# Second blocks that begin with the latent input, and blocks that begin and end by token block

## The reference

```python
def second_layer(x, ...):
    h = rmsnorm(x, norm_w)
    (m_cq, m_ckv, m_kr, m_gate, g_q, g_k, g_v, g_z, g_b, g_a,
     c_q, c_k, c_v, c_gate) = jnp.split(h @ w_in, split_points, axis=-1)
    y_mla = mla_mixer(m_cq, m_ckv, m_kr, ...) * silu(m_gate)
    y_gdn = gdn_mixer(g_q, g_k, g_v, g_z, g_b, g_a, ...)
    y_moba = moba_mixer(c_q, c_k, c_v, t5_table) * silu(c_gate)
    return x + concatenate([y_mla, y_gdn, y_moba]) @ w_out
```

## Time and profile before

| | |
|---|---|
| median of 3 runs | 1325.55 us |
| profiled execution, its own time | 1327.21 us |
| its span, first to last instruction | 1325.4 us |
| mean granted clock of TensorE | 0.997 |
| TensorE busy | 1301.4 us |
| VectorE busy | 1026.0 us |
| ScalarE busy | 746.5 us |
| weights and data read | 220.88 MB |

### The profile page before, as it was taken

The page is one execution under the profiler, slowest core; times in us unless marked ns, Lnnn a source line. Parts: engine busy times, 40 slices in busy tenths (PEclk is TensorE's granted clock), DMA queues, the critical chain, the costliest instruction groups (busy, mean ns, idle before and its releaser), DMA issues. The chain is left out here.

```text
span 1325.4 us, 26400 instructions
## 1 busy us (share of the span) xinstructions
PE 1301.4 (98%) x10796; PEld 1240.3 (94%) x10796; DVE 1026.0 (77%) x1763; ACT 746.5 (56%) x1149; POOL 47.3 (4%) x48
## 2 busy tenths in 40 slices
PE   9999999999999999999999999999999999999997
PEld 8899999999999999999999989999989899888996
DVE  6899998677777677999997768777778746677565
ACT  6544566556454465544757556544567445586364
POOL 0000000000000000100000000000001100001100
PEclk9999999999999999999999999999999999999999
DMA  8565455565555465646365555665654223343232
GB/s 279 190 201 181 160 161 189 163 220 186 196 191 191 153 229 176 215 162 197 126 210 167 197 184 178 207 203 193 206 163 152 64 97 128 122 143 112 81 101 75
DMA packets 108991, 223.62 MB, mean 169 GB/s; under 512 B 6180, under 2 KB 17700, under 8 KB 108872
## 3 DMA queue, kind: packets, MB, share of 16 engines
q1 hardware_dynamic: 106736, 218.99, 49.5%
q10 hardware_dynamic: 2136, 2.96, 0.7%
HBM read 220.88 MB, written 1.06 MB: 167 GB/s over the span
## 5 line engine op out<-in xcount | busy, mean ns | idle before, releaser
L1191 ACT ACTIVATE whi<-ring 128x1024 fp32r<-128x1024 f32 (+3 forms) x430 | 433.7, 1027 | 343.2 <-PE bank L513 221.3
L1764 DVE TENSOR_TENSOR wlo<-ring,whi 128x1024 fp32r<-128x1024 f32 (+3 forms) x430 | 496.9, 1180 | 166.0 <-ACT whi L1191 133.1
L513 PE MATMUL bank<-hhi,whi 128*128 128x256 f32 x2016 | 272.5, 277 | 2.5 <-ACT hhi L1228 1.8
L522 PE MATMUL bank<-hhi,wlo 128*128 128x256 f32 x2016 | 273.0, 277 | 1.0 <-DVE wlo L1764 1.0
L513 PE MATMUL bank<-hlo,whi 128*128 128x256 f32 x2016 | 269.1, 276 | 0.0
L513 PEld LDWEIGHTS bank<-hhi,whi 128*128 128x128 f32 x2016 | 248.3, 192 | 5.5 <-issue 3.9
L522 PEld LDWEIGHTS bank<-hhi,wlo 128*128 128x128 f32 x2016 | 246.9, 192 | 4.9 <-issue 3.2
L513 PEld LDWEIGHTS bank<-hlo,whi 128*128 128x128 f32 x2016 | 247.3, 193 | 0.0
L1932 DVE SCALAR_TENSOR_TENSOR w<-w,par 128x256 f32<-128x256 f32 x240 | 98.1, 479 | 0.0
L535 PE MATMUL bank<-whi,hhi 128*128 128x512 f32 (+2 forms) x256 | 93.1, 366 | 0.0
L535 PE MATMUL bank<-whi,hlo 128*128 128x512 f32 (+2 forms) x256 | 92.6, 364 | 0.0
(11 more groups left out here) (311 smaller groups left out, 1549.1 us busy)
## 6 DMA issues: line engine op xcount, KB each, us to landing
ring<-in_w_in SPq DMA_DIRECT2D x100, 1024.0 KB, 5.1
ring<-in_w_ffn_down SPq DMA_DIRECT2D x22, 1024.0 KB, 5.1
ring<-in_w_ffn_gate SPq DMA_DIRECT2D x20, 1024.0 KB, 5.1
ring<-in_w_ffn_up SPq DMA_DIRECT2D x20, 1024.0 KB, 5.2
ring<-in_w_merge SPq DMA_DIRECT2D x8, 1024.0 KB, 5.2
ring<-in_w_out SPq DMA_DIRECT2D x8, 1024.0 KB, 5.0
ring<-in_w_oc SPq DMA_DIRECT2D x4, 1024.0 KB, 5.3
ring<-in_w_od SPq DMA_DIRECT2D x4, 1024.0 KB, 5.2
```

What stands on the lines that cost most here:

```text
L513: done = e.matmul(o, wh[:, k, cols(u)], paired(s_[:, k0 + k, :]), stop=False, skip_group_check=True, start=opens and k == 0 and s_ is sh a ...
L522: done = e.matmul(o, wl[:, k, cols(u)], paired(sh[:, k0 + k, :]), start=False, stop=closes, skip_group_check=True)
L1191: e.activation(part_of(whi, j), part_raw(j), ACT.Copy).then_inc(*up("hi.a"))
L1764: e.tensor_tensor(part_of(wlo, j), part_raw(j), part_of(whi, j), ALU.subtract).then_inc(*up("lo.v"))
```

## The change

What it does:

- The order of a second block's input is `m0`, `kc`, `cqk`, `qc`, `vc`, `mg`, `cvg`, `z`. The eight gate columns are columns 416 to 423 of `m0`; the part `ba`, its products and the turning of its result are gone. `TWO_PLAN` has new places for all steps; `MIX_PLAN` is the same.
- The first group of each block takes all four parts' high products for token block 0 first, then for token block 1 (`chans_first`, `toks_first`); the transposes of token block 1 lie inside.
- A block ends by token block over its last two pairs of parts (`last_pairs`); the next block's transposes of token block 0 lie before the last part.
- The norm is done by token block, on 128x512 at a time, with gains read as rows (`rowg`, a 512 KB transfer per norm on ScalarE's queue). Fillers are left at the start of the kernel only.
- High and low activations of the first channel groups go to two halves of a bank, which ScalarE copies and VectorE adds.
- A group takes a bank when its first product needs it (`Held`). The normalization of probabilities (`probs_v`) is a step of its own, after the next logits.
- The bias inputs are loaded during the last feed-forward block.

The core of the diff:

```diff
-TWO_IN = (("kc", 1184, 1696), ("ba", 2720, 2728), ("qc", 672, 1184), ("m0", 0, 416), ("vc", 1696, 2208),
-          ("cqk", 2728, 3240), ("cvg", 3240, 3752), ("mg", 416, 672), ("z", 2208, 2720))
+TWO_IN = (("m0", 0, 424), ("kc", 1192, 1704), ("cqk", 2728, 3240), ("qc", 680, 1192), ("vc", 1704, 2216),
+          ("mg", 424, 680), ("cvg", 3240, 3752), ("z", 2216, 2728))
...
-        "bias": [5, 5, 5, 6],
-        "taps": [12, 20, 34],
-        "others": [28, 34, 41, 41, 53],
-        "decay": [10, 10, 11, 12],
-        "delta": [17, 18, 20, 20, 30, 30, 36, 37, 39, 41, 43, 46, 46, 48, 48, 50, 51, 52, 53, 54, 55, 62, 65, 66, 66],
-        "latent": [26, 29, 30, 34, 36, 37, 39, 43, 46, 53, 54, 65, 66],
-        "outs": [58, 66, 71, 71],
+        "bias": [4, 5, 6, 7],
+        "taps": [16, 33, 41],
+        "silu": [19, 36, 44],
+        "others": [38, 42, 47, 48, 51],
+        "decay": [8, 11, 12, 13],
+        "delta": [22, 23, 25, 25, 28, 29, 32, 33, 35, 37, 39, 41, 43, 45, 46, 48, 49, 50, 52, 53, 54, 60, 63, 64, 64],
+        "latent": [9, 16, 20, 27, 31, 34, 40, 44, 46, 52, 55, 62, 63],
+        "outs": [57, 65, 69, 69],
...
+            def turn_norm(name, l, tb):
+                for g in range(2):
+                    bk = ps.take(e, "s", "nT", name, l, tb, g)
+                    e.wait_ge(*at("xn", name, l, tb, g))
+                    for i in range(4):
+                        done = turn(bk[:, cols(i)], xn[:, tb, cols(4 * g + i)])
...
+            def last_pairs(j, acc, pairs, tag, l, following):
+                for tb in range(2):
+                    for n, ((sh, sl), k0, ready) in enumerate(pairs):
+                        for nh in range(2):
...
+                            elif n == 1 and nh == 1 and following:
+                                turn_norm(*following, 0)
...
+            def chans_first(j, held_of, name, l, mid, after):
...
+                for i in range(4):
+                    e.wait_ge(SEM["hi.a"], j + i + 1)
+                    e.wait_ge(*at("hlo", name, l, 0, i // 2))
+                    products(i, 0, (0, 1))
+                    if i == 3 and not begins:
+                        turn_norm(name, l, 1)
+                    products(i, 0, (2, 3))
+                for i in range(4):
+                    e.wait_ge(*at("hlo", name, l, 1, i // 2))
+                    products(i, 1, range(4)).then_inc(*up("first.p"))
+                    mid(j + i)()
+                    low_ready(j + i)
...
+            def toks_first(j, held, n, name, l, mid, after):
...
+                for i in range(4):
+                    e.wait_ge(SEM["hi.a"], j + i + 1)
+                    e.wait_ge(*at("hlo", name, l, 0, i // 2))
+                    high(i, 0)
+                low_ready(j)
+                low(0, 0)
+                turn_norm(name, l, 1)
...
             def decay_p(l):
-                yield 0
-                bk = ps.take(e, "s", "bg", l)
-                e.wait_ge(*at("rows8", l))
-                for tb in range(2):
-                    done = turn(bk[:, 8 * tb:8 * tb + 8], rows8[:, cols(tb)])
...
                 yield 2
                 bk = ps.take(e, "s", "gsum", l)
-                awake(bk, 6)
                 e.wait_ge(*at("gv", l))
...
+            def norm_a(name, l, x_in, j0):
+                square_a(name, l, x_in, 0)
+                split_to(j0 + 2)
+                high_a(name, l, 0, 0)
+                high_a(name, l, 0, 1)
+                square_a(name, l, x_in, 1)
+                split_to(j0 + 3)
+                scale_a(name, l, xn)
+                high_a(name, l, 1, 0)
+                high_a(name, l, 1, 1)
...
+                for nh in range(2):
+                    add(0, nh)
+                    weigh(0, nh)
                 sums_v(name, l, 0)
+                for g in range(2):
+                    scale_v(name, l, 0, g, xn)
+                split_to(j0)
+                add(1, 0)
+                low_v(name, l, 0, 0)
+                add(1, 1)
+                low_v(name, l, 0, 1)
                 sums_v(name, l, 1)
+                weigh(1, 0)
+                weigh(1, 1)
+                scale_v(name, l, 1, 1, xn)
+                split_to(j0 + 1)
+                low_v(name, l, 1, 0)
+                split_to(j0 + 2)
+                low_v(name, l, 1, 1)
...
                         logits_v(name, l, tb, tag, lgm, 1.0, (mask_mla, mask_moba)[i], 96 + 16 * tb, rowtiles=i == 1)
+                        if tb:
+                            probs_v(name, l, 0, tag, lgm, 96)
+                    yield 7 + 4 * i
+                    probs_v(name, l, 1, tag, lgm, 112)
```

More of the change, by code:

```diff
@@ L574, in norm_p @@
-            def norm_p(name, l):
-                e.wait_ge(SEM["init.v"], 1)
-                for tb in range(2):
[L578 to L588, removed]
+            def turn_norm(name, l, tb):
+                for g in range(2):
+                    bk = ps.take(e, "s", "nT", name, l, tb, g)
+                    e.wait_ge(DMA["id"], 16)
+                    e.wait_ge(*at("xn", name, l, tb, g))
+                    for i in range(4):
+                        done = turn(bk[:, cols(i)], xn[:, tb, cols(4 * g + i)])
+                    done.then_inc(*up("norm.p"))
+                    put("norm.p", "nT", name, l, tb, g)
@@ new lines, in toks_first, with high, low @@
+            def toks_first(j, held, n, name, l, mid, after):
+                def high(i, tb):
+                    wh = part_of(whi, j + i)
+                    for k in range(2):
+                        for s_ in hh:
+                            done = e.matmul(held[tb][:, 0:n], s_[:, 2 * i + k, cols(tb)], paired(wh[:, k, 0:n]), stop=False,
+                                            start=i == 0 and k == 0 and s_ is hhi, skip_group_check=True)
+                    return done
+                def low(i, tb):
+                    wl = part_of(wlo, j + i)
+                    for k in range(2):
+                        done = e.matmul(held[tb][:, 0:n], hhi[:, 2 * i + k, cols(tb)], paired(wl[:, k, 0:n]), start=False,
+                                        stop=i == 3, skip_group_check=True)
+                    return done
+                for i in range(4):
[4 more added lines that the diff above has]
+                low(0, 0)
+                turn_norm(name, l, 1)
+                for i in range(4):
+                    e.wait_ge(*at("hlo", name, l, 1, i // 2))
+                    high(i, 1).then_inc(*up("first.p"))
+                    mid(j + i)()
+                    low_ready(j + i)
+                    if i:
+                        low(i, 0)
+                    low(i, 1).then_inc(*up("second.p"))
+                    after(j + i)
@@ L758, in mix_p @@
                 for name, kind, n, _ in MIX_IN:
-                    held = [ps.take(e, "m", name, l, i) for i in range(2)]
+                    if name == "glu_b":
+                        chans_first(j, lambda u: ps.take(e, "m", name, l, u), "mix", l, between, behind)
+                        j += 4
+                        put("second.p", name, l)
+                        continue
+                    held = [ps.take(e, "s" if name == "glu_a" else "m", name, l, i) for i in range(2)]
                     for i in range(4):
[L761 to L764, removed]
+                        (chans if kind == "chans" else toks)(j, held, n, hh, 2 * i, i == 0, i == 3, between(j))
                         behind(j)
@@ L2204, in ffn_v @@
                         last = [None] * 2
-                        e.wait_ge(*at("gpad", l, i6, i))
+                        if i6:
+                            e.wait_ge(*at("gpad", l, i6, i))
+                        else:
+                            for u in range(2):
+                                g2 = two(gpad[:, i, u, 2:258])
+                                e.wait_ge(*at("gate_high", l, 2 * i + u))
+                                e.tensor_tensor(g2, g2, sides(bank("gate", l, 0, 2 * i + u))[1], ALU.add).then_inc(*up("ffn.v"))
+                                leave("ffn.v", "gate", l, 0, 2 * i + u)
+                            e.wait_ge(*now("ffn.v"))
                         for k3 in range(3):
```

480 lines of the change are left out of this document (263 added, 217 removed).

## The result

The changed kernel takes 1370.59 us (median, 1369.44 to 1372.61), the one before 1326.33: a ratio of 1.0333 with an interval of 1.0313 to 1.0353, so 44 us slower. Forecast was slower, at 1349 with a range up to 1358. The sign and the waits were right; the size was not.

The account below looks back on a forecast made before the run. TensorE, busy 98% of the span, was taken as the bound. Removed work and old waits (-19.1), new waits (+42.2) and clock (0) made net +23.1 on 1325.55, so 1349 us; range 1310 to 1358.

Parts of the forecast that it names:

- (a): Decay sums, place 12: TensorE waits 4.2 us for its operand, 5.2 in layer 0; 9.4 over both layers.
- (b): First inverse step, place 28: TensorE waits 1.3 us for VectorE's queue; 2.6 over both layers.
- (e): Second delta block, place 54: waits 1.7 us for the state's copy behind a split; 3.4 over both layers.
- (f): Second bank of `z`: waits 4.8 us for ScalarE's copy of the first values behind exponentials; 9.6 over both layers.
- (c): Fourth inverse product, place 43: waits 5.4 us for a ScalarE and VectorE chain ending in a subtraction; 10.8 over both layers.
- (d): Turned probabilities, place 44: wait 2.6 us for token block 1's split-off normalization; 5.2 over both layers.
- (g): Place 62: waits 0.6 us for the last normalization; 1.2 over both layers.
- Rival C: Clock adds: six waits over 4 us each bring a half-clock stretch of 1.7 us, net +7, 1355 us; chance 0.12.
- A: Table holds: ScalarE and VectorE come early enough, all new waits vanish, the saved 19.1 stay, 1306 us; chance 0.20.
- B: Half of the waits: only (a), (f) and scraps, 19 to 24 us; 1325 to 1330, no difference; chance 0.13.
- D: Boundaries don't gain: ScalarE's square of token block 1 is held up by a split (1.06); 1353 us; chance 0.05.
- E: Token block 0's high products wait for both blocks' norms, boundaries cost 3 us more each; 1363 us; chance 0.02.

Follow-up runs that it names:

- run 8: The kernel before, with its old input order and blocks, given a new table of places from the same search walk: 1324.6 us, ratio 0.9987.
- run 6: The changed kernel with only another table of places, found by a search over a walk of all engines: 1307.7 us, ratio 0.9871 to the kernel before.
- run 2: The changed kernel with fillers that fit: 20 before the decay sums, 9 before the third inverse product, 19 before z's first product: 1357.4 us.
- run 5: The changed kernel with a table of places made by hand, each long wait taken apart by moving a step or two: 1358.7 us, ratio 1.0239.
- run 4: The changed kernel with latent step 10, the other attention's logits for token block 1, at place 56 instead of 55: 1359.0 us, ratio 1.0241.
- run 1: The changed kernel with fillers before four long waits of each second block (40, 18, 34, 38), each taking twice the time assumed: 1390.9 us.
- run 7: The changed kernel with a second searched table of places, which misplaces two bias steps so it computes something else: 1309.6 us, ratio 0.9880.

## Why the prediction was wrong, point by point

**Boundaries, +1.15 us each, right.** The same product of the two first layers starts at 178.84 and 658.10 before:

```profile
178.84 0.91 PE L513 MATMUL bank<-fhi,whi 128*128 128x256 f32 x6 [1.04 <-DVE w L2178]
658.10 0.57 PE L513 MATMUL bank<-fhi,whi 128*128 128x256 f32 x3 [1.04 <-DVE w L2178]
```

and after:

```profile
179.08 0.68 PE L521 MATMUL bank<-fhi,whi 128*128 128x256 f32 x4 [1.05 <-DVE w L2320]
656.01 0.68 PE L521 MATMUL bank<-fhi,whi 128*128 128x256 f32 x4 [1.04 <-DVE w L2320]
```

Two boundaries lie between: 479.26 against 476.93, 1.17 us each. The result is right, but the working behind it is not: the terms of the chain that the forecast lists add up to 5.8 us, not to "some 5.1". The trace shows why the smaller sum came out all the same:

```profile
311.70 0.69 DVE L1877 TENSOR_TENSOR x<-bank,x 128x512 f32<-128x512 f32 x1 [0.28 <-PE bank L589]
...
313.26 1.29 DVE L1937 TENSOR_TENSOR xn<-x,rowg 128x512 f32<-128x512 f32 x2
313.42 0.95 POOL L2744 TENSOR_TENSOR st<-st,mhalf 128x1 f32<-128x1 f32 x1 [5.40 <-DVE st L1883]
...
316.57 0.69 DVE L1890 TENSOR_TENSOR hboth<-bank,hboth 128x512 fp32r<-128x512 f32 x1 [0.29 <-ACT hboth L1279]
```

Only one addition stands in the chain and the weighing runs beside GpSimd's power, while that power takes 0.95 us for 0.56. From 311.70 to 317.26 it is 5.56 us, against 5.1 and 0.5 of handing over: luck, in part. The boundaries in front of the second blocks, forecast at 0.7 each, were not read apart; TensorE waits 1.0 us for the low halves in each (L644 waiting for L1890, 2.0 in both), where the forecast left 2.0.

The first norm was forecast to cost 0.3. The same product starts 0.24 us later than before in this pair. But over all profiled runs with the new blocks it starts between 178.43 and 179.24, and in run 8, with the old ones, at 179.16: no cost is shown.

**The saved 19.1 us, right within 2 as a sum.** Run 6 has the whole change with few waits left and is 17 below. Its parts were not measured one by one: run 6 still has 5 us of side waits (3.4 and 1.8 in the list above), and it has lost the two stretches at half clock of the kernel before.

**The waits, right in sum by luck.** Forecast +42.2; the eight lines of the list above sum to 45.2. But the seven waits that were forecast come to 36.0 of it, and 9.2 are two that were missed. (a) 9.4 against 9.3, (b) 2.6 against 2.5, (e) 3.4 against 3.0, (f) 9.6 against 9.0. (c) was forecast at 10.8 and is 8.0, because the stretch at half clock before it lengthens TensorE's own work: in run 2, where fillers keep the clock up in front of it, it is 11.3. (d) and (g) together were forecast at 6.4 and are 4.2. Of the two that were missed, the first is GpSimd's, which takes a power of 1.63 us just ahead of the mask that the third inverse product needs. The mask ends at 1256.63, and the product starts at 1256.73:

```profile
1253.77 1.63 POOL L2744 TENSOR_TENSOR st<-st,mhalf 128x8 f32<-128x8 f32 x1 [15.45 <-DVE st L2510]
1255.37 1.26 POOL L2804 TENSOR_TENSOR w<-w,cst 128x512 f32<-128x512 f32 x1
```

Step 0 of `others` is at place 38 and the mask's step at 37 to 39; I had walked GpSimd's queue for the latent only. The other is at the second output, whose sources are 2.2 us late: `outs` step 1, at place 65, stands behind the two scaling steps of place 64. In run 5, which has it at 64, this wait is 1.1.

**The clock, wrong.** This is the step that failed: "I assume as many afterwards: 0", two stretches of 3.4 us as before. There were ten, seven of them of 6.8 us. The term that was put at 0 is about 20 us by the pitch of the products (changed kernel against run 6), and run 2 gave 13 of it back by fillers alone. With it the forecast's own sum is 1349 + 20 = 1369, against 1370.6. Rival C had the mechanism, at 1.7 us for each of six waits less what is there, +7, with a chance of 0.12: too low in number (waits of 2.2 us can bring a stretch too), in length (mostly 6.8, not 3.4) and in chance. The row for it was at hand: a wait of 1.3 us behind 1.3 us of fillers already had a stretch behind it. With 40 us of new idle time forecast, most of it in pieces of over 4 us, no added low clock was the less likely assumption. A small slip besides: chains 25% longer give 1359, not 1358, as the upper end.

**The other rivals.** A (the table holds) fell, and so did B: (a) and (f) alone are 18.3 us of the 45.2. D and E fell with the boundaries' measured gain.

**The rule on table loads.** The Trainium skill's page "ScalarE: Activation LUTs", section "What ACT_TABLE_LOAD costs", gives each load a drain of some 1.38 us behind it; by an estimate from that figure wait (a) would have been 2.8 us longer. The rows above have the activation that needs the table 1.29 us after the load's start (1183.01, then 1184.30), and the wait is 4.5 us in the first layer and 4.8 in the second, forecast 5.2 and 4.2 without the drain. The trace shows no drain, and going by the row was right.

**The rule on banks.** The Trainium skill's page "Perfetto Trace Analysis", section "Optimizing Tensor Performance", asks that independent groups rotate through different banks, so that the copying out of one overlaps the next. In (f) the banks did rotate, and TensorE still waited 4.5 us in each layer, since the copy stood behind the exponentials. Moving these behind the copy (run 4) gave 11.6 us for 9.0 of wait: the rotation helps only if the copy itself is in time.

## What to carry to other kernels

Where an order of steps is fixed by hand and TensorE is busy 98% of the time, a new order of the stream can invalidate the whole table of places: walk all engines, GpSimd's queue too, before judging the change by its table. Price a new wait of TensorE of 2 us or more at its length and, as an estimate from this kernel (about 20 us for ten waits), another two us for the clock. Fillers that fit into the waits gave 13 us of that back here, and are a quick test of how much of a loss the clock is. Judge the idea and the table apart: here the idea was worth 17 us and the table that came with it cost 63.

## What was not expected of the hardware

Inside the runs, stretches at 1.2 GHz came in two lengths, 3.4 and 6.8 us; one in the hand-made table (run 5) lasted 10.2 us. The length of a wait does not fix the length of the stretch: in the changed kernel the wait of 2.2 us for the third inverse product has one of 6.8 us in the first layer and of 3.4 in the second, and the wait of 2.2 us at the outputs has one in both layers there, in one layer in run 2 and in none in run 1. Short waits can have one too: run 7 has one of 3.4 us in each layer with no wait over 1.3 us. What brings them in one case and not in another stays open. A us at half clock cost only 0.3 us here (run 2), not 0.5. Part of this is that ScalarE and VectorE catch up meanwhile: wait (c) is 5.6 us in run 2 and 4.0 in the changed kernel.
